# Gate table from one shared bf16 comparison, spread over eight expert tiles instead of twelve

## The reference

```python
    best_s, best_pos = lax.top_k(cand_s, PEER_TOPK)
    best_i = jnp.take_along_axis(cand_i, best_pos, axis=-1)
    gate = jax.nn.softmax(best_s, axis=-1)
    ...
        u = jnp.take(expert_u, ib, axis=0)
        act = jax.nn.gelu(jnp.einsum('td,tkd->tk', xb, u).astype(jnp.float32), approximate=False)
        vv = jnp.take(expert_v, ib, axis=0)
        return jnp.einsum('tk,tkd->td', (gb * act).astype(h.dtype), vv)
```

## Time and profile before

| | |
|---|---|
| time, median of 3 runs | 3132.37 us (3130.73 to 3136.59) |
| profiled execution, span | 3134.2 us (the page gives the span; the times of the runs are those above) |
| TensorE busy | 2990.2 us, 95% of the span |
| VectorE busy | 2025.2 us, 65% |
| ScalarE busy | 1261.6 us, 40% |
| GpSimd busy | 1157.7 us, 37% |
| mean granted clock of TensorE | 0.979 |

### The profile page before, as it was taken

How to read it: one execution, slowest core, us unless ns; L and a number is a source line. 1 busy time by engine, 2 the same in 40 slices (tenths; PEclk the granted TensorE clock), 3 DMA queues, 4 the chain that set the end, 5 groups by cost and what they waited for, 6 DMA issues and landing times.

```text
span 3134.2 us, 47541 instructions
## 1 busy us (share of the span) xinstructions
PE 2990.2 (95%) x17673; PEld 2612.4 (83%) x17673; DVE 2025.2 (65%) x3238; ACT 1261.6 (40%) x2075; POOL 1157.7 (37%) x564
## 2 busy tenths in 40 slices
PE   6999999998999999999999999899999998999998
PEld 3766679998988888888887788699999975799986
DVE  4767515999977778788886255466651375466622
ACT  3347333446963333333333334432222446432221
POOL 2420333664014444455553222044444430244442
PEclk9998999999999999999999999799999999999999
DMA  6710223555679999999996211023223420122231
GB/s 247 280 60 1 62 93 96 166 175 191 227 248 350 346 328 341 337 351 350 346 347 229 75 55 41 14 88 94 87 88 101 117 81 1 41 89 93 94 101 67
DMA packets 179876, 509.22 MB, mean 162 GB/s; under 512 B 14881, under 2 KB 72353, under 8 KB 175393
## 3 DMA queue, kind: packets, MB, share of 16 engines
q1 hardware_dynamic: 72288, 262.57, 25.4%
q0 software_dynamic: 37440, 136.40, 11.9%
q10 hardware_dynamic: 70016, 108.54, 10.3%
HBM read 467.60 MB, written 39.85 MB: 162 GB/s over the span
## 4 chain that ended last, share of the span: by engine, by line
PE 87%; ACT 5%; DVE 4%; issue 2%; DMA 1%; ACTq 0%; DVEq 0%
PE ps L1279 23%; PE ps L1230 17%; PE ps L1167 16%; PE ps L1533 8%; PE ps L901 8%; ACT arena L1960 2%; PE ps L1351 2%; PE ps L952 1%; ACT arena L1976 1%; PE ps L1680 1%; PE ps L1299 1%; PE ps L1457 1%; PE ps L1414 1%; PE ps L654 1%; PE ps L1421 1%
## 5 line engine op out<-in xcount | busy, mean ns | idle before, releaser
L2314 POOL TENSOR_TENSOR w_lo<-ring,w_hi 128x1024 fp32r<-128x1024 f32 x300 | 755.0, 2520 | 1387.9 <-ACT w_hi L795 1387.8
L795 ACT ACTIVATE w_hi<-ring 128x1024 fp32r<-128x1024 f32 x500 | 525.4, 1055 | 771.9 <-PE ps L1230 277.4
L1230 PE MATMUL ps<-w_hi,arena_r 128*128 128x512 f32 x1536 | 426.8, 397 | 4.5 <-DVE arena_r L2772 4.5
L1167 PE MATMUL ps<-h_hi,w_hi 128*128 128x384 f32 x1024 | 355.5, 347 | 5.0 <-issue 5.0
L1230 PEld LDWEIGHTS ps<-w_hi,arena_r 128*128 128x128 f32 x1536 | 289.0, 189 | 72.2 <-DVE arena_r L2772 5.0
L1167 PE MATMUL ps<-h_lo,w_hi 128*128 128x384 f32 x1024 | 348.9, 341 | 0.0
L1279 PE MATMUL ps<-h_hi,w_hi 128*128 128x264 f32 (+2 forms) x1536 | 347.5, 298 | 0.6 <-DVE arena L2869 0.5
L1167 PE MATMUL ps<-h_hi,w_lo 128*128 128x384 f32 x1024 | 346.4, 338 | 0.0
L1279 PE MATMUL ps<-h_lo,w_hi 128*128 128x264 f32 (+2 forms) x1536 | 346.2, 297 | 0.0
L1279 PE MATMUL ps<-h_hi,w_lo 128*128 128x264 f32 (+2 forms) x1536 | 345.6, 297 | 0.0
L2327 POOL DMA_INDIRECT arena<-u_rows,arena x128 | 193.4, 1511 | 375.8 <-DVE arena L2748 354.5
(11 more groups left out here) (343 smaller groups left out, 5444.0 us busy)
## 6 DMA issues: line engine op xcount, KB each, us to landing
ring<-weight_stream SPq DMA_DIRECT2D x500, 512.0 KB, 3.7
gates<-arena ACTq DMA_DIRECT2D x12, 2048.0 KB, 7.3
arena<-gates ACTq DMA_DIRECT2D x32, 768.0 KB, 14.3
arena<-w_modulation ACTq DMA_DIRECT2D x17, 1024.0 KB, 5.3
early_acts<-arena ACTq DMA_DIRECT2D x64, 192.0 KB, 2.7
arena<-early_acts ACTq DMA_DIRECT2D x32, 384.0 KB, 7.7
arena<-w_modulation ACTq DMA_DIRECT2D x2, 2560.0 KB, 15.0
x<-x_t ACTq DMA_DIRECT2D x1, 2112.0 KB, 19.5
```

The costliest lines, as they stand in the source:

```text
L795: act.activation(w_hi[:, s, :], ring[:, s, :], ACT.Copy).then_inc(hi_ready, 1)
L1167: last = pe.matmul(ps[:, bank, 0:ND], w, v, start=c == 0 and p == 0, stop=c == DC - 1 and p == 2)
L1230: last = pe.matmul(ps[:, Y_BANKS[b][half], :], a[u], w[v][:, half * BANK:(half + 1) * BANK], start=first and p == 0, stop=final and p == 2)
L2314: pool.tensor_tensor(w_lo[:, s, :], ring[:, s, :], w_hi[:, s, :], ALU.subtract)\
```

## The change

Both one-hots of a group now come from one bf16 comparison on VectorE: `idx12` holds both indices, `hot[g % 2]` both results, [2, 128 keys, 8 tokens]. ScalarE only widens the second one into `hot2` (`widen_hot`, one copy of 1024 elements); VectorE scales all eight tokens of the first into `hot1g` (`scale_keys`). Both now read in order and write words that are 512 bytes apart. `key_of` is made before the routing. VectorE's order is scale g, compare g + 1. The table goes between the chunks of eight tiles (54 to 61), one or two batches per chunk. Tile 52 stands ahead of the last `indices`, 53 behind it, 62 and 63 behind the loop. VectorE makes a low part after every sixth group and the last four behind the loop. Behind it, ScalarE fetches the gates first and waits for one save of each activation buffer, for all of them only after the first two late tiles.

```diff
 GROUP = 2 * BATCH
 QUAD = 4 * STEP
 GBUFS = 6
-SCALED = 4
+G_TILES = 8
+G_FIRST = 54
 DOT_STEPS = NSEL // 8
 LOG_SEQ = 9
 PADS = 5
...
         yg = view(1056, D)
         routed = [view(1056 + 384 * k, 3, NSEL) for k in range(2)]
         pos_abf = view(1824, 2, NSEL)
-        idx2 = view(2112, ND)
         gate_t = view(2496, ND)
-        idx1 = place("idx1", [P, ND], BF16, at=at_arena + 2880)
+        idx12 = place("idx12", [P, 2, ND], BF16, at=at_arena + 2880)
+        key_of = place("key_of", [P, NKEYS, GROUP], BF16, at=at_arena + 3776)
         eidx = view(3264, NSEL, dt=U32)
         gate_g = view(3392, NSEL)
         act_g = view(3520, NSEL)
...
         g_stage = [view(4448 + 4096 * k, NKEYS, STEP) for k in range(2)]
         hot2 = view(12640, 2, GROUP, NKEYS)
         hot1g = view(14688, 2, GROUP, NKEYS)
-        hot1 = [place(f"hot1_{k}", [P, NKEYS, GROUP], BF16, at=at_arena + 16736 + 512 * k) for k in range(2)]
-        key_of = place("key_of", [P, NKEYS, GROUP], BF16, at=at_arena + 17760)
+        hot = [place(f"hot{k}", [P, 2, NKEYS, GROUP], BF16, at=at_arena + 16736 + 1024 * k) for k in range(2)]
         g_rows = [view(19552 + D * k, D) for k in range(GBUFS)]
         early = view(4448, 2, 2, ND)
...
         routed_ready = sem("routed_ready")
         eidx_ready = sem("eidx_ready")
         hot1_made = sem("hot1_made")
-        hot_scaled = sem("hot_scaled")
+        hot_widened = sem("hot_widened")
         rows_in = [sem(f"rows_in{k}") for k in range(GBUFS)]
         rows_used = sem("rows_used")
         dots_taken = sem("dots_taken")
...
             for b in range(1, TB):
                 span(pe, INDEX_TURNS[b - 1], INDEX_TURNS[b], early_turn)
+                if b == TB - 1:
+                    early_tile(G_TURN, 0)
                 indices(b)
+            early_tile(G_TURN, 1)
             pe.wait_ge(h_row_ready, 1)
-            def g_batch(n, group, k):
-
-                pe.wait_ge(hot_ready, group + (k // 2 + 1))
-                pe.wait_ge(hot_scaled, group + (k // 2 + 1))
-                wait(pe, g_kept, n + (k - 3))
+            def g_batch(k):
+
+                pe.wait_ge(hot_ready, k // 2 + 1)
+                pe.wait_ge(hot_widened, k // 2 + 1)
+                wait(pe, g_kept, k - 3)
                 for t in range(BATCH):
                     at_t = BATCH * (k % 2) + t
                     last = pe.matmul(ps[:, k % 4, t * P:(t + 1) * P], hot2[:, k // 2 % 2, at_t, :],
                                      hot1g[:, k // 2 % 2, at_t, :], start=True, stop=True)
                 last.then_inc(g_made, 1)
-            def g_steps(i):
-                for s in range(RING):
-                    early_tile(i + G_TURN, s, lambda k: g_batch(i * 32 + DC * s, i * 16 + 4 * s, k))
-            turns(pe, 3, g_steps)
+            def g_between(j):
+
+                def batches(c):
+                    per = G_BATCHES // G_TILES
+                    for k in range(per * c // DC, per * (c + 1) // DC):
+                        g_batch(per * j + k)
+                return batches
+
+            for j in range(G_TILES):
+                early_tile((G_FIRST + j) // RING, (G_FIRST + j) % RING, g_between(j))
+            for t in range(G_FIRST + G_TILES, TILES):
+                early_tile(t // RING, t % RING)
             def late_tile(i, j, turn, s):
                 wait(pe, gelu_done, i * 2 + (TILES + j - 1))
...
                 act.activation(best[b % 2], best[b % 2], ACT.Exp).then_inc(gate_exp, 1)
-            def scale_hot(g):
-
-                act.wait_ge(hot1_made, g + 1)
+            def widen_hot(g):
+
+                act.wait_ge(hot1_made, g + 2)
                 wait(act, g_made, 2 * (g - 1))
-                for t in range(SCALED):
-                    k = GROUP * g + t
-                    last = act.activation(hot1g[:, g % 2, t, :], hot1[g % 2][:, :, t], ACT.Identity,
-                                          scale=gate_t[:, k:k + 1])
-                last.then_inc(hot_scaled, 1)
+                act.activation(hot2[:, g % 2].rearrange("p t j -> p j t"), hot[g % 2][:, 1], ACT.Copy).then_inc(hot_widened, 1)
             groups = ND // GROUP
-            scale_hot(0)
+            for t in range(G_TURN * RING, G_FIRST):
+                early_gelu(t // RING, t % RING)
+            widen_hot(0)
             for g in range(groups):
                 step, n = g // 4, 2 * g
                 if g % 4 == 0:
                     wait(act, g_saved[step % 2], 16 * (step // 2))
                 if g + 1 < groups:
-                    scale_hot(g + 1)
+                    widen_hot(g + 1)
                 for k in (n, n + 1):
-                    if k % DC == DC - 1:
-                        early_gelu(G_TURN + step // RING, step % RING)
+                    per = G_BATCHES // G_TILES
+                    if k % per == per - 2:
+                        early_gelu((G_FIRST + k // per) // RING, (G_FIRST + k // per) % RING)
                     act.wait_ge(g_made, k + 1)
                     act.activation(g_stage[step % 2][:, :, BATCH * (k % DC):BATCH * (k % DC + 1)],
                                    ps[:, k % 4, :].rearrange("p (t i) -> p i t", i=NKEYS), ACT.Copy).then_inc(g_kept, 1)
...
                     act.wait_ge(g_kept, n + 2)
                     act.dma_start(gates_d[:, step, :], g_stage[step % 2].rearrange("p i t -> p (i t)"))\
                         .then_inc(g_saved[step % 2], 16)
+            for t in range(G_FIRST + G_TILES, TILES):
+                early_gelu(t // RING, t % RING)
             def fetch_gates(q):
...
             for k in range(2):
                 act.wait_ge(g_saved[k], 16 * (STEPS // 2))
-                act.wait_ge(act_saved[k], 16 * (TILES // 2))
             fetch_gates(0)
+            for k in range(2):
+                act.wait_ge(act_saved[k], 16)
             fetch_acts(0)
             for j in range(2):
                 late_gelu(0, j, used(t0, j))
             for j in range(2):
                 high_gated(j, late_hi[:, 0, j, :], late[:, j, :])
+            for k in range(2):
+                act.wait_ge(act_saved[k], 16 * (TILES // 2))
             for i in range(last_step):
                 k0 = 2 + 6 * i
                 p = i % 2
...
             def keep(b):
                 dve.wait_ge(routed_t, b)
-                for k, dst in enumerate((idx1, idx2, gate_t)):
+                for k, dst in enumerate((idx12[:, 0], idx12[:, 1], gate_t)):
                     dve.tensor_copy(dst[:, (b - 1) * P:b * P], ps[:, 6, k * P:(k + 1) * P]).then_inc(routed_kept, 1)
             steps = [0]
...
                     dve.scalar_tensor_tensor(eidx, to[:, 0, :], float(NKEYS), to[:, 1, :], ALU.mult, ALU.add)\
                         .then_inc(eidx_ready, 1)
+            dve.tensor_copy(key_of[:, :, :], cst("iota").unsqueeze(2).broadcast_to([P, NKEYS, GROUP])).then_inc(hot1_made, 1)
             for b in range(TB):
                 route_block(b)
                 if b == TB - 1:
...
                     keep(b - 1)
             keep(TB - 1)
-            def hot_group(g):
+            def compare_keys(g):
                 t = slice(GROUP * g, GROUP * (g + 1))
-                wide = [P, GROUP, NKEYS]
-                iota = cst("iota").unsqueeze(1).broadcast_to(wide)
-                wait(dve, hot_scaled, g - 1)
-                dve.tensor_tensor(hot1[g % 2][:, :, :], idx1[:, t].unsqueeze(1).broadcast_to([P, NKEYS, GROUP]), key_of[:, :, :],
-                                  ALU.is_equal).then_inc(hot1_made, 1)
+                both = [P, 2, NKEYS, GROUP]
+                wait(dve, hot_widened, g - 1)
+                dve.tensor_tensor(hot[g % 2][:, :, :, :], idx12[:, :, t].unsqueeze(2).broadcast_to(both),
+                                  key_of[:, :, :].unsqueeze(1).broadcast_to(both), ALU.is_equal).then_inc(hot1_made, 1)
+
+            def scale_keys(g):
+
+                t = slice(GROUP * g, GROUP * (g + 1))
+                dve.wait_ge(hot1_made, g + 2)
                 wait(dve, g_made, 2 * (g - 1))
-                dve.tensor_tensor(hot2[:, g % 2], idx2[:, t].unsqueeze(2).broadcast_to(wide), iota, ALU.is_equal)
-                dve.wait_ge(hot1_made, g + 1)
-                rest = slice(GROUP * g + SCALED, GROUP * (g + 1))
-                dve.tensor_tensor(hot1g[:, g % 2, SCALED:, :], hot1[g % 2][:, :, SCALED:].rearrange("p j t -> p t j"),
-                                  gate_t[:, rest].unsqueeze(2).broadcast_to([P, GROUP - SCALED, NKEYS]), ALU.mult)\
-                    .then_inc(hot_ready, 1)
+                dve.tensor_tensor(hot1g[:, g % 2].rearrange("p t j -> p j t"), hot[g % 2][:, 0],
+                                  gate_t[:, t].unsqueeze(1).broadcast_to([P, NKEYS, GROUP]), ALU.mult).then_inc(hot_ready, 1)
             def low_early_slot(k):
...
                     .then_inc(lo_ready, 1)
             dve.wait_ge(routed_kept, 3 * (TB - 1))
```

(16 more changed lines are left out.)

## The result

The changed kernel takes 3155.55 us (median; 3150.7 to 3158.16) against 3131.8 for the kernel before: a ratio of 1.0068, 95% interval 1.005 to 1.0085. It is slower by 24 us, less than 1% but clear of the interval; 26 us faster was forecast, and the time lies outside the range.

What follows compares the result with a forecast made beforehand. In the gate table TensorE's matmuls waited for one-hots from ScalarE and VectorE. Loop 121.8 instead of 151.7 us, start 0.6 later, behind 1.55 longer, 1.7 taken off: 26 us faster, 3106.4 us, range 3100 to 3142.

Steps and rivals of the forecast that it cites:

- I take 1.06: ScalarE's widening copy of 1024 elements per group: scattered write costs nothing extra, 1.06 us, the low end.
- I take 1.22, for the reason above: VectorE's scaling of 1024 elements per group: scattered write costs nothing extra, 1.22 us, the low end.
- the high end: New writes cost what scattered reads cost: VectorE's scaling 2.00 us, ScalarE's widening 2.74 us.
- Rival 1: Gate table loop: scattered writes cost as much as scattered reads, scaling 2.00 us, time 3141 us; chance 0.19.
- The range's upper end: Top of the forecast time range for the whole kernel, 3142 us.
- The comparison of 2048: VectorE's single bf16 comparison per group, in place of two: 1.22 us for 2048 elements.
- rival 2: VectorE's double comparison isn't run at the bf16 rate: 2.29 us, time 3153 us; chance 0.04.
- TensorE's 14.92 us per tile: TensorE in the loop: a tile with 12 batches takes 14.92 us, 119.4 us for eight tiles.
- VectorE's chain of 2.38 us: VectorE in the loop: scaling 1.13 plus comparison 1.25 us, 2.38 us per group.
- rival 3: Loop engines too level, each waiting on the next: 12 us of the gain go, 3118 us; chance 0.11.
- The start: Stretch before the loop, tiles 52 and 53 ahead: first batch at 751.0 us, not 750.4.
- Behind the loop: From the loop's end to the first share of the expert sums: 26.3 us, 1.55 longer than before.

Runs made afterwards that it cites:

- k9: Kernel before, with its first one-hot in two halves of four tokens, so scalings read bf16 words 8 bytes apart instead of 16; 3125.6 us.
- k1: Changed kernel with both new writes in order instead of 512 bytes apart, the reordering left out (products read wrongly ordered one-hots); 3118.2 us.
- k10: Changed kernel with the comparison laid out in pairs of keys, so widening and scaling write runs of two f32 words; 3117.3 us.
- k2: Changed kernel with both new writes in order and TensorE reading its operands 32 bytes apart; 3212.5 us.
- k5: Changed kernel's places with the one-hots of before, scaling split over GpSimd (four tokens), ScalarE (two) and VectorE (two); 3155.6 us.
- k8: Kernel before, with GpSimd scaling five tokens of a group, ScalarE three, VectorE none, and the key table made early; 3147.5 us.
- k6: Only the changed one-hots, in the places of the kernel before (twelve tiles in the loop, none ahead or behind); 3148.9 us.
- k11: One-hots of k10 in the places of the kernel before (twelve tiles, nothing ahead or behind); 3122.9 us.

## Why the prediction was wrong

**The step that failed** is the choice between the ends for both new writes: "I take 1.06" and "I take 1.22, for the reason above". The reason was that the copy into the stage reads single words 512 bytes apart and pays nothing. But those reads are in PSUM, and the copy's writes to SBUF come in runs of four words. I took the row "nearest for order on the output side", though its output was not in single words. The nearest for what costs was the scattered SBUF read of the same loop, which I used as the high end: 2.00 us for the scaling, measured 2.03. For the widening the high end of 1.98 (the same 0.9 ns more) was right, 2.06 measured; 2.74, from ScalarE's scaling, had the scale operand in it, and k9 leaves only 0.94 ns per element of its 1.65 to the jump. k1 and k10 show that with cheap writes the loop comes within 2.6 and 3.4 us of the forecast.

**Rival 1 was the case that came.** Its loop, 752 to 909.4, is 157.4 us; measured 158.1. Its time, 3141, fell short by 14.6 us: 2.2 at the start, 0.7 in the loop, 2.9 behind it and 1.8 at the first share's clock. The other 7 us stay open. In the profiled execution 4.7 of them lie ahead of the routing; k1, k2 and k5 run the same code up to there and did not have them, so they come and go between executions. Its chance of 0.19 was too low: the line rule of the Trainium skill (SBUF — State Buffer, Specifications (TRN2)) does not set reads and writes apart, the trace agreed with that rule for reads on two engines, and against it stood a row of another memory. The writes now agree too: 2.03 us single, 1.22 in order, 1.23 in runs of two words. The range's upper end was rival 1's point value with nothing above it.

**What held.** The comparison of 2048 (1.24 against 1.22) and rival 2's refusal; TensorE's 14.92 us per tile, nearly level with VectorE and with cheap one-hots the bound (k1's 124.5 us against 119.4 of work); VectorE's chain of 2.38 us (k1's scalings start at 792.85, 795.23 and 797.63); and rival 3's small chance: the level engines cost each other some 3 us, not 12.

**The start** was forecast with the first batch 0.6 us later, measured 3.8. Two pieces of the chain that ended last, and then ScalarE's time line:

```profile
741.01 3.73 POOL w_lo L2329
744.88 5.98 PE ps L1167 x24
```

```profile
755.46 0.49 ACT L1943 ACTIVATE arena<-ps 128x384 f32<-128x384 f32 x1 [3.12 <-PE ps L1167]
755.84 1.05 ACT L795 ACTIVATE w_hi<-ring 128x1024 fp32r<-128x1024 f32 x1
...
756.79 3.69 ACT L1969 ACTIVATE arena<-hot 128x1024 f32<-128x1024 bf16 x2
```

The low part of tile 52 began when forecast (741.01 less the 4.7 us shift is 736.3) but took 3.7 us, not the 2.7 that I had from dividing the merged row of four. In the kernel before, too, the first of the four alone took 3.72, and the other three the rest. Each time a VectorE operation with two inputs in SBUF was running when it began (735.48 to 737.77 before, 740.22 to 742.51 here), and it ended 2.2 us after that one: here GpSimd waits for VectorE, as VectorE waits for GpSimd in k8. Then TensorE ran the tile partly at the lower clock (granted 0.72), behind 2 us without work: 6.0 us for 4.2. I had no row for a clock that falls in so short a wait, and let the tile run at full speed. The transposes were held up by it, VectorE's first comparison began at 751.95, and ScalarE's GELU of tile 53 came at 755.46, with the widening behind it, as said, but 0.9 us longer by its write. So of the 3.2 us over the forecast about 1.1 are the low part's, 1.8 the clock's and 0.9 the widening's, less 0.6 since the transposes took 0.3 us where I had 0.9.

**Behind the loop** 26.3 us were forecast, 29.3 measured. The save in the chain that ended last, then the time lines:

```profile
918.06 9.86 DMA gates<-arena
```

```profile
928.00 1.86 ACTq L1998 DMA_DIRECT2D arena<-gates  x2
...
938.31 1.03 DVE L2787 TENSOR_TENSOR arena<-arena 128x384 f32<-128x384 f32 x2 [10.18 <-DMA arena<-gates]
```

I had the GELU and high part of tile 63 as what sets the fetch. They ended at 926.87, even a little early. But the save of the last gates, issued at 918.06, landed only after 9.86 us, and so ScalarE issued the fetch at 928.00, 11.1 us behind the loop (10.2 forecast). VectorE used it 10.3 us later, where I carried over 8.1. The profiles split cleanly: with nothing moved behind the loop (before, k6, k8, k9, k11) the fetch follows the save by 7.6 us and is used 8.1 to 8.9 us later; with early tiles there (the other nine) it is 8.7 to 10.1 and 9.6 to 12.3. So both transfers that the stretch waits for are longer with the tiles there that I had moved as cover for TensorE. The tiles' activation saves stand in the same queue of ScalarE's, and their weights move on the same DMA engines, busy for 0.88 of this stretch; which of these does it, or whether the new order of the fetches has a part, no run tells. TensorE then does wait, 2.3 us at its end, and the clock of the first step is lower for it. I had costed the five microseconds of idle time as gone and nothing as taking their place.

## What to carry to other kernels

A reordering costs about the same whether it stands in the read or in the write: single SBUF words (bf16 read 16 bytes apart, f32 written 512 bytes apart) took about 0.8 ns more each on VectorE and 0.9 to 1.0 ns on ScalarE. So lay out the small type such that every access goes in runs or steps of 8 bytes, before work is moved between engines; that alone turned 24 us lost into 18 won. And a row bounds a cost only in the memory in which it was taken: the SBUF read had the price of the SBUF write, the PSUM read had not.

## What the runs showed of the hardware

- f32 words written to SBUF 512 bytes apart: 1024 took 1.98 to 2.03 us on VectorE and 2.06 on ScalarE, against 1.22 and 1.06 in order. In runs of two words: 1.23 and 1.18.
- Reads of bf16 words: 512 took 1078 ns at 16 bytes' distance, 685 at 8 (VectorE); 128 took 522 and 402 ns (ScalarE, with a scale operand).
- TensorE's f32 operands 32 bytes apart: loads 338 ns instead of 192, matmuls 420 instead of 275.
- VectorE operations with two SBUF tensors that began while a GpSimd tensor operation ran ended only after it: 0.69 us became 2.05, 1.22 became 2.60; one that began 0.15 us ahead of GpSimd's kept its 1.21 us. The other way round, GpSimd's low part, 2.3 us at its shortest, took 3.72 us when it began inside such a VectorE operation.
- With early tiles behind the loop, a 2 MB save of gates took 8.7 to 10.1 us until its data could be fetched, in nine profiles; without them 7.6, in five.
